# A recurrent decoder step: how often the small matmuls of branches C and B break into TensorE's stream

## What is computed

```python
h = rmsnorm(x, norm_pre)                       # 288 tokens x 2048
p = split_cols(h @ w_in)                       # all branches' inputs
# branches B and C, per head, chunk by chunk:
b = jnp.cumsum(gi, axis=2)                     # log forget gates
inter = jnp.einsum("nhtk,nhkv->nhtv", qi * jnp.exp(b), S)
att = jnp.einsum("nhtk,nhsk,nhtsk->nhts", qi, ki, decay)
intra = jnp.einsum("nhts,nhsv->nhtv", att, vi)
S_new = jnp.exp(b_last)[..., None] * S + jnp.einsum(
    "nhsk,nhsv->nhkv", ki * jnp.exp(b_last[:, :, None] - b), vi)
# o = rmsnorm(inter + intra); each branch times its SiLU gate, then
pb = jnp.einsum("ntcw,cwd->ntcd", branches, w_branch)
gate = jax.nn.sigmoid(h @ w_merge)
merged = (gate * pb).sum(branches)
x = x + rmsnorm(merged @ w_out, norm_post)
```

## Time and profile before

| | |
|---|---|
| three runs | 1867.18, 1869.22, 1869.27 us, median 1869.22 |
| span of the profiled execution | 1866.1 us from first to last instruction |
| what lies around the span | at most 3.1 us against the median |
| TensorE busy | 1846.4 us, 99% |
| VectorE, ScalarE, GpSimd busy | 1251.9, 904.3, 463.0 us |
| branch C's heads | from about 523 to 867 us of the span |
| branch B's heads | from about 867 to 1272 us |

### The profile page before, as it was taken

The page is one execution under the profiler, slowest core; times in us unless marked ns, Lnnn a source line. Parts: engine busy times, 40 slices in busy tenths (PEclk is TensorE's granted clock), DMA queues, the critical chain, the costliest instruction groups (busy, mean ns, idle before and its releaser), DMA issues.

```text
span 1866.1 us, 39932 instructions
## 1 busy us (share of the span) xinstructions
PE 1846.4 (99%) x16782; PEld 1789.2 (96%) x16782; DVE 1251.9 (67%) x2224; ACT 904.3 (48%) x1336; POOL 463.0 (25%) x768
## 2 busy tenths in 40 slices
PE   7999999999999999999999999999999999999998
PEld 6999999999999999999999999999999999999986
DVE  7655568877777677765888888787556655544544
ACT  6533345454464544445565666664443333433433
POOL 5676887778810000000000000002111100000000
PEclk9999999999999999999999999999999999999999
DMA  6887776555554554545445554555655554655542
GB/s 248 301 266 267 245 243 198 179 177 187 176 200 158 185 192 142 203 139 201 156 160 183 172 171 161 173 171 199 222 174 181 198 176 148 216 188 162 191 182 85
DMA packets 95523, 353.25 MB, mean 189 GB/s; under 512 B 12896, under 2 KB 13168, under 8 KB 91632
## 3 DMA queue, kind: packets, MB, share of 16 engines
q1 hardware_dynamic: 76608, 279.48, 44.3%
q0 software_dynamic: 14128, 50.60, 8.2%
q10 hardware_dynamic: 4608, 20.62, 3.2%
HBM read 323.21 MB, written 27.44 MB: 188 GB/s over the span
## 4 chain that ended last, share of the span: by engine, by line
PE 96%; DVE 2%; ACT 0%; DMA 0%; issue 0%; SPq 0%; DVEq 0%; ACTq 0%
PE ps L1884 95%; DVE w_lo L1212 1%; DMA raw<-in_w 0%; PE ps L2219 0%; ACT w_hi L704 0%; PE ps L2079 0%; DVE o_y L1218 0%; DVE xc L1218 0%; PE ps L2112 0%; SPq L416 0%; DVE norm L1206 0%; DVE norm L1257 0%; PE ps L2003 0%; PE ps L1997 0%; PE ps L2080 0%
## 5 line engine op out<-in xcount | busy, mean ns | idle before, releaser
L1884 PE MATMUL ps<-h_hi,w_hi 128*128 128x288 f32 x2944 | 877.7, 299 | 4.1 <-ACT h_hi L704 2.5
L1884 PE MATMUL ps<-h_hi,w_lo 128*128 128x288 f32 x2944 | 866.5, 295 | 0.0
L1884 PE MATMUL ps<-h_lo,w_hi 128*128 128x288 f32 x2944 | 861.5, 294 | 0.0
L1212 DVE TENSOR_TENSOR w_lo<-raw,w_hi 128x1024 fp32r<-128x1024 f32 x496 | 622.3, 1266 | 280.0 <-ACT w_hi L704 277.0
L704 ACT ACTIVATE w_hi<-raw 128x1024 fp32r<-128x1024 f32 x496 | 520.5, 1056 | 438.8 <-PE ps L1884 388.1
L1884 PEld LDWEIGHTS ps<-h_hi,w_hi 128*128 128x128 f32 x2944 | 552.1, 188 | 10.8 <-issue 6.7
L1884 PEld LDWEIGHTS ps<-h_hi,w_lo 128*128 128x128 f32 x2944 | 552.7, 188 | 1.3
L1884 PEld LDWEIGHTS ps<-h_lo,w_hi 128*128 128x128 f32 x2944 | 552.4, 188 | 0.5 <-DVE h_lo L1212 0.5
L1884 PE MATMUL ps<-br_hi,w_hi 128*128 128x288 f32 x640 | 192.2, 300 | 0.0
L1884 PE MATMUL ps<-br_hi,w_lo 128*128 128x288 f32 x640 | 188.9, 295 | 0.0
L1884 PE MATMUL ps<-br_lo,w_hi 128*128 128x288 f32 x640 | 188.3, 294 | 0.0
(11 more groups left out here) (408 smaller groups left out, 2290.5 us busy)
## 6 DMA issues: line engine op xcount, KB each, us to landing
raw<-in_w SPq DMA_DIRECT2D x496, 512.0 KB, 4.1
w_out<-in_w SPq DMA_DIRECT2D x24, 512.0 KB, 5.2
acc<-in_kc ACTq DMA_DIRECT2D x8, 1024.0 KB, 5.8
vc<-in_vc ACTq DMA_DIRECT2D x8, 1024.0 KB, 6.3
w_scratch<-st_wide POOLq DMA_DIRECT2D x40, 128.0 KB, 4.3
a_w<-w_scratch POOLq DMA_DIRECT2D x8, 640.0 KB, 7.5
b_scratch<-st_wide POOLq DMA_DIRECT2D x32, 128.0 KB, 4.0
c_S<-in_gla POOLq DMA_DIRECT2D x4, 1024.0 KB, 8.1
```

What stands on the lines that cost most here:

```text
L1212: return dve.tensor_tensor(out, a, b, ALU.subtract)
L1884: return pe.matmul(out, a, b, start=start, stop=stop)
```

## The change

In C the nine interruptions become four. The first line of a head's code moves into the head before it, ahead of that head's fourth D gate block, as `gate_ranks(i + 1)`; head 0 keeps its own at the start. Both `turn_values` stand just ahead of `all_pairs`, behind the gate block. Both `mixed` stand together. `updates(i, 2, 0)` moves behind branch block 4i+1, next to `sum_squares`. `updates(i, 2, 1)` moves behind branch block 4i+2, next to `gate_ranks`. In B `turn_values` moves from ahead of block `hg` to behind the second C gate block, just ahead of `all_pairs`. The transposed values get other places in PSUM (banks 5, 6 and 7). On ACT `split_values` stands behind `turned_keys`. On DVE, in C, `weigh("D", 4 * i + 1)` goes ahead of `new_states(0)` and `own_values(1)`, and the second `new_states` goes behind `upto(u0 + 23)`. The number and size of matmuls stay the same.

```diff
@@ PSUM places of the transposed values
             if v == 0:
-                return ps[:, 2:4, 0:P], ps[0:3 * TS, 4, 0:P]
-            return ps[:, 7, 0:2 * P].rearrange("p (a c) -> p a c", a=2), ps[0:3 * TS, 7, 2 * P:3 * P]
+                return ps[:, 6, P:3 * P].rearrange("p (a c) -> p a c", a=2), ps[0:3 * TS, 6, 3 * P:4 * P]
+            return ps[:, 7, 2 * P:4 * P].rearrange("p (a c) -> p a c", a=2), ps[0:3 * TS, 5, 3 * P:4 * P]
@@ ACT, C head
-                split_values(i, 2, vals, 0)
                 upto(u0 + 12)
                 gate("D", 4 * i)
                 upto(u0 + 13)
                 turned_keys(i, 2)
+                split_values(i, 2, vals, 0)
+                split_values(i, 2, vals, 1)
                 upto(u0 + 14)
...
-                split_values(i, 2, vals, 1)
@@ ACT, B head
                 gate("C", 2 * i)
-                split_values(i, 1, vals, 0)
...
                 turned_keys(i, 1)
+                split_values(i, 1, vals, 0)
@@ TensorE, turn_values
-                if v == 0 and (i or nv == 1):
-                    wv("out", 0)
-                    w("new", 1, 0)
-                    w("Sp", 1, 0)
-                if v:
-                    w("kT", 4, 1)
+                if v == 0:
+                    w("X")
+                    if i or nv == 1:
+                        wv("out", 0)
+                        w("new", 1, 0)
+                        w("Sp", 1, 0)
@@ TensorE, all_pairs
-                w, _ = heads_of(i, nv)
-                w("X")
-                pe.wait_ge(S("g_vT"), 2 * heads_before(i, nv)[1] + 2)
@@ TensorE, B head
                 gate("C", 2 * i)
-                turn_values(i, 1, h_values, 0, ("hi", i))
                 h("hg", i)
                 gate("C", 2 * i + 1)
+                turn_values(i, 1, h_values, 0, ("hi", i))
                 all_pairs(i, 1, h_values)
```

More of the change, by code:

```diff
@@ L926, in split_values @@
             def split_values(i, nv, vals, v):
-                _, wv = heads_of(i, nv)
-                wv("vt", v + 1)
                 by_token, of_samples = turned(v)
@@ L1652, in _ @@
                 sg(add(vals[4][:, 0], vals[4][:, 0], vals[4][:, 1]), "c_added")
+                upto(u0 + 20)
+                weigh("D", 4 * i + 1)
                 new_states(i, 2, vals, 0)
                 own_values(i, 2, vals, 1)
-                upto(u0 + 20)
-                weigh("D", 4 * i + 1)
                 upto(u0 + 21)
                 outputs(i, 2, vals)
+                upto(u0 + 23)
                 new_states(i, 2, vals, 1)
-                upto(u0 + 23)
                 low_outputs(i, 2, vals, br0_hi, br0_lo)
@@ L2079, in turn_values @@
                     pe.transpose(by_token[:, tt], vals[1][:, v, tt * P:(tt + 1) * P], ident[:])
-                sg(pe.transpose(of_samples, vals[1][:, v, SEQ:T + 2 * TS], ident[:]), "g_vt")
+                pe.transpose(of_samples, vals[1][:, v, SEQ:T + 2 * TS], ident[:])
             def pairs(tok):
@@ L2147, in sum_squares, with gate_ranks @@
                 sg(mm(ps[:, 7, 0:T], ones[:], vals[4][:, 0]), "g_ssq")
-            for i in range(4):
[L2151 to L2157, removed]
+            def gate_ranks(i):
+                sg(mm(ps[:, 7, 0:T], g_wu[:, i], c_r), "c_z")
+            pe.wait_ge(S("g_params"), 48)
+            pe.wait_ge(S("c_r"), 2)
+            gate_ranks(0)
+            for i in range(4):
                 h("ck", i)
@@ L2161, in _ @@
                 h("cv", 2 * i + 1)
-                turn_values(i, 2, c_values, 0, ("cv", 2 * i))
                 gate("D", 4 * i)
+                for v in range(2):
+                    turn_values(i, 2, c_values, v, ("cv", 2 * i + v))
                 all_pairs(i, 2, c_values)
                 h("cg", 2 * i)
-                turn_values(i, 2, c_values, 1, ("cv", 2 * i + 1))
                 h("cg", 2 * i + 1)
-                mixed(i, 2, c_values, 0)
+                for v in range(2):
+                    mixed(i, 2, c_values, v)
                 if i == 0:
@@ L2171, in _ @@
                 branch("D", 4 * i)
-                mixed(i, 2, c_values, 1)
                 gate("D", 4 * i + 1)
+                branch("D", 4 * i + 1)
                 updates(i, 2, 0)
-                branch("D", 4 * i + 1)
                 sum_squares(i, 2, c_values)
                 gate("D", 4 * i + 2)
+                branch("D", 4 * i + 2)
                 updates(i, 2, 1)
-                branch("D", 4 * i + 2)
+                if i < 3:
+                    pe.wait_ge(S("g_rstd"), i + 1)
+                    gate_ranks(i + 1)
                 gate("D", 4 * i + 3)
```

## The result

| | before | after |
|---|---|---|
| median | 1867.77 us (21 runs, 1866.58 to 1869.74) | 1870.64 us (21 runs, 1869.58 to 1872.10) |
| span of the profiled execution | 1866.1 us | 1869.6 us |
| TensorE busy | 1846.4 us | 1846.9 us |

The ratio of after to before is 1.0015, 95% interval 1.0008 to 1.0021: the changed kernel is 1.5 to 3.9 us slower. Forecast were 1871.4 us and +2.2 us.

The account below looks back on a forecast made before the run. TensorE, busy 1846.4 of 1866.1 us, was taken to bound the kernel. Terms 0.0 + 2.2 + 0.0 = +2.2 us on 1869.2 gave 1871.4 us (+0.12%), with an 8-in-10 range of 1867.6 to 1874.4.

Parts of the forecast that it names:

- Term 1: TensorE, 27 fewer interruptions in B and C: no fee per interruption, so 0.0 us, bounds -0.5 to +0.5.
- The fee rival: TensorE: each of 27 interruptions pays a fee, 0.10 us in and 0.10 out, 5.4 us saved; chance 0.06.
- Its neighbour in the Trainium skill: TensorE: a constant of about 166 ns paid once per interruption, by estimate 27 x 0.166 = 4.5 us saved.
- The bound of 0.10 for the two `mixed`: C heads, joined `mixed`: at most one change of form saved or paid per head, 4 x 0.10 = 0.4 us either side.
- Term 2: B's transposes leave a place hidden by the wait at `hg`'s second unit: 7 heads x 0.32 = +2.2 us.
- the waits give it back: B heads: DVE starts its chain earlier or the low part follows TensorE, 0.32 us not lost, 1869.2 us; chance 0.10.
- Term 3: Branch C, regrouped DVE and ACT work: no new wait on TensorE, 0 us; `g_X` has 1.0 us to spare.
- the slower rival: C: DVE late to `g_X`, TensorE waits up to 2.8 us in three heads, 8.4 us, 1879.8 us; chance 0.12.

Follow-up runs that it names:

- x9: Kernel before plus seven extra 128x128 transposes in each B head's second C gate block, at seven separate places; 1874.46 us against 1868.50, ratio 1.0033.
- x10: Kernel before plus seven extra 128x128 transposes in each B head's second C gate block, all at one place; 1874.60 us, ratio 1.0035.
- x1: Kernel before with only branch C's part of the change; 1868.45 us against 1867.86, ratio 1.0003.
- x6: Kernel before with branch B's three transposes of values per head left out on TensorE, and ACT's wait for them; 1868.00 us against 1868.18, ratio 0.9998.
- x7: Kernel before with the DVE scan making B's `g_b` issued twice, between the squares and the low part for `hg`; 1874.98 us, ratio 1.0033.
- x8: Kernel before with a second DVE scan into `g_b` per B head, placed behind the low part for `hg`; 1868.23 us, ratio 1.0001.
- x3: Changed kernel with, in B on DVE, the low part of a head's second unit moved behind the first three gate operations; 1868.07 us, ratio 0.9999.
- x4: Kernel before with, in B on DVE, the low part of a head's second unit moved behind three gate operations; 1866.97 us against 1867.86, ratio 0.9994.
- x2: Kernel before with only branch B's part of the change; 1870.75 us against 1867.86, ratio 1.0016.

## Why the prediction was right

**Base.** The three runs that stood ahead had their median at 1869.22; 21 runs have it at 1867.77. The forecast of 1871.4 lies 0.8 us above the measured 1870.64, while its difference of +2.2 lies 0.7 below the measured +2.9, inside the interval. So the total came out this near partly by luck: a base 1.45 us too high was offset by a difference too small. The span rose by 3.6 us, of which 1.16 are the start of the program; what happens there differs between executions and not between the kernels.

**Term 1, the fee: right to be nothing, small and of the other sign in fact.** The sum had 0.0 with bounds of 0.5. C's heads took 0.03 us more with five interruptions fewer each, 0.006 us a join, as much as x9 against x10 show. Over four heads that is 0.13 us. Rows 3, read to hundredths, couldn't show it. Why a join loses these nanoseconds wasn't asked. The fee rival, 5.4 us, falls with x9 and x10, and for C's own joins with x1. Its neighbour in the Trainium skill (page "TensorE: Matmul & The Clock Gate", section "Single matmul latency") puts about 166 ns on top of the streaming time of a single bf16 matmul; by that, an estimate, x9 would be some 8 us slower than x10. The trace disagrees: x9 is no slower. The bound of 0.10 for the two `mixed` was too wide as well: 3.68 us apart and together.

**Term 2, the transposes: the mechanism and the size.** Forecast were a wait of 0.46 and heads of 51.02 us in seven heads; the profile after has 0.44 and 51.02, and 7 x 0.32 = 2.2 of the 2.25 us that B's region gained. That the wait hid them was argued from rows; x6 shows it, since leaving them out changes nothing, and x7 and x8 show that the wait belongs to DVE's chain. The rival "the waits give it back" is out by the heads of 51.02, and the only version that gives it back is one where DVE's chain is shortened (x3).

**Term 3, waits in C: right.** The whole region lies 1.16 us later in this profile. Less that, the states came at 590.58 - 1.16 = 589.42 (the sum had 589.4) and the low part behind them ended at 595.12 - 1.16 = 593.96 (the sum had 594.3); no matmul waited for it. `g_X` had 1.06 us to spare where 1.0 was said. No carry into the next head came about, so the slower rival (from 1.0 us of carry on) didn't start.

**What stays open.** How the 2.9 us of the medians divide beyond the 2.4 that heads account for (2.25 and 0.13) can't be told: the interval is 1.5 to 3.9. The medians of the kernels with C's new order lie above their partners with the old one by 0.6 us (x1 against the kernel before) and 1.1 us (x3 against x4). Neither is clear of noise, and whether C's order costs more than the 0.13 us of its heads isn't shown.

## What to carry to other kernels

Before joining small matmuls, look for a wait that starts behind one of them. Work of TensorE that stands ahead of a wait for another engine costs nothing as long as some of that wait is left and the other engine's chain doesn't hang on the work: here 0.33 us of transposes stood free ahead of a wait of only 0.13. Moving it behind the wait makes it cost what it takes. The test is cheap: take the work out where it stands, and if nothing gets faster, leave it there, or shorten the other engine's chain first. In this dense stream, the number of places at which small matmuls break in was nothing to optimise by itself.

## What the runs showed that was not expected

**A hidden wait doesn't show as one.** In the kernel before TensorE is on 96% of the ending chain and its table of waits counts two waits for low parts, none of them in branch B, yet in seven heads DVE set the period. A delay of 0.13 us lies inside the overlap of two records (0.29 us long, 0.13 apart), and only distances from start to start show it. Lengthened to 0.44 it shows, as 0.18.

**Single stalls without a named cause.** In three of the 13 profiled executions (x1, x2, x3) one stretch in B takes longer, in one head only. Of x1 and of x3, TensorE, one behind the pairs and one within them:

```profile
1212.33 0.38 PE L1883 MATMUL ps<-br_hi,w_hi 128*128 128x288 f32 x1
1213.04 0.40 PE L1883 MATMUL ps<-br_hi,w_lo 128*128 128x288 f32 x1 [0.33 <-issue]
```

```profile
1160.92 0.19 PE L1883 MATMUL ps<-g_X 128*32 128x32 f32 x1 [0.67 <-issue]
```

They cost 0.6 and 0.8 us (that head 51.29 in place of 50.70, and 51.37 in place of 50.55). The one of x2 costs 0.35 us (51.37 in place of 51.02), at the same instruction of the same head as x1's, and shows no idle time. No semaphore is waited for; what holds the instruction back was not looked into. They are about as large as the differences asked about here, and that is one reason to read the length of a head, seven times over, and not only the span.
